# Layer 1's first two input tiles as split products in banks of their own, two buffers for turned powers, an output product that waits block by block, and a GLU tile loaded ahead of the moves

## The chip, the cores and the metric

The kernel runs on one core of one Trainium2 chip. The metric is the device time of one execution in microseconds (us); the median over several executions is what counts. A change of under 0.3% is taken here as one that a measurement of this kernel can't tell from none.

## What is computed

Two layers of a diffusion backbone over 256 latent tokens with a prefix of 256 context tokens, model width 1024, everything in f32. Cut to what matters here:

```python
for l in range(2):
    a = rmsnorm(h, norm1_g[l]) * (1 + sc1) + sh1          # context and latent tokens
    p = a @ w_in[l]                                       # columns: fourier | ssm | gate a | gate b
    y_ssm = s5_branch(p_ssm)                              # diagonal complex scan, both directions
    y_a = fourier_mix(p_fourier) @ w_four
    y_b = (y_ssm @ w_glu_a) * sigmoid(y_ssm @ w_glu_b)
    h = h + g1 * ((sigmoid(p_ga) * y_a + sigmoid(p_gb) * y_b) @ w_out)
    f = rmsnorm(h, norm2_g[l]) * (1 + sc2) + sh2
    h = h + g2 * (swiglu(f) if l == 0 else moe_top2_of_8(f))
out = rmsnorm(h, final_g)
```

In layer 1 the context tokens only feed the scan's starting state, so there the scan input is computed for all 512 tokens and everything else for the 256 latent ones.

## The kernel before, in words

Activations lie transposed: features on the partitions, 512 tokens along the row (`NT`), in eight blocks of 128 features (`KD`). Every dense product makes one block of 128 output features for all tokens in one PSUM bank, with up to eight matmuls that add up over the input blocks. Each engine has one hand-written instruction list, and semaphores join them; nothing is ordered by a scheduler. `dense(...)` and `side(...)` at the top of `program` give each product a bank and a turn, and `place`, `bank_for`, `arrived` and `taken` turn these into semaphore waits.

**Loads.** SP issues the weight tiles (2 MB each) in the order of the list `stream` into a ring of three slots. A tile may be issued once the last product that used the tile three places before it is done (`ring_load`, `last_use`). The list `moves` is `stream` with the reshaping moves that go through DRAM in between: `pack_load` (the scan input, written to `uds` by ACT in `stage_u`, read back in another layout into `pack`), `toep_load`, and `ys_move` (scan output from `stage` to `yds` and back into `pack`). SP is one queue in order: a wait of one entry holds up all that follow.

**Two kinds of product.** `product` multiplies f32 by f32; the trace shows two matmul instructions for each such matmul. `split_product`, used in layer 0's feed-forward part, takes a tile apart into a high part (ACT copies it rounded to fp32r, `weights_high`, into `FWH`) and the rest (DVE subtracts, `weights_low`, into `ringl`, which lies on the same memory as the ring slot), does the same with the activations (`aTh`, and `aTl` on the memory of `aT`), and adds three products: high by high, high by low, low by high, one matmul instruction for each. `FWH` has two buffers.

**Layer 1's head.** After layer 0's last residual, PE sums the squares (`sums`), ACT takes the root, DVE inverts, PE spreads it (`inverse_rows`); DVE scales the eight blocks (`norm`) and ACT adds the shift (`shift`). Then PE makes "u" (scan input, tile `w_in` 1, 512 columns) and "f" (Fourier input, tile `w_in` 0, 256 columns) with `product`, block after block; ACT copies each block of u out and stores it to `uds`. When all four are stored, SP issues the eight `pack` loads and then `bp` 1, the second of two tiles of turned powers. PE next makes the scan's E blocks from `pack` with `bp` 0 (blocks 0 and 1) and `bp` 1 (blocks 2 and 3), then the Fourier transforms, the gates ga and gb, the scan output Y, `ya`, `glub`, `glua` and `out`. DVE scans after the E blocks.

**Turned powers.** Layer 1's `bp` tiles are made in layer 0 among the `ya` products: DVE makes a set of powers (`in_powers`), PE transposes it (`turn`, L1595), ACT copies it from two banks into `BWs` (`turned`, L696) and stores it to `bps` (L701). There are eight sets and one `BWs`, so ACT waits before each set until the store before it has landed. ACT's next work behind the eighth set is the evacuation of layer 0's `glub` products, which alternate between two banks. `out_powers` on DVE (L1182) waits for all eight stores, since its buffer lies on the memory of `BWs`.

**Output product.** DVE mixes the two branches block by block (`mix_ready`, L1349 to L1353); PE waits for all eight mixed blocks before the first `out` matmul.

```python
                pe.wait_ge(mix_ready, 8 * l + 8)
                for h in range(2):
                    w = slot(("w_out", l, h))[:].rearrange("p (k c) -> p k c", k=KD)
```

After layer 1's `out` comes the expert part, about half of the time, which the change doesn't touch.

Of the kernel before, what the change touches and what calls it, by code (L numbers as in the profile page):

```python
# [22 lines left out]
F32 = mybir.dt.float32  # L23
# [82 lines left out]
def program(nc, a, out, bps, cks, gds, uds, yds):  # L106

    top = ExitStack()
    with top:
# [48 lines left out]
        bw_stored = sem("bw_stored")  # L158
# [15 lines left out]
        a_high = sem("a_high")  # L174
        w_high = sem("w_high")
# [47 lines left out]
        for part, size in enumerate(PARTS):  # L223
            for m in range(part * PARTS[0], part * PARTS[0] + size):
# [3 lines left out]
        dense([("ss", 1, 0), ("inv", 1, 0)] + blocks_of(1, ("u", "f", "ga", "gb", "ya", "glub", "glua", "out")) + [("ss", 1, 1), ("inv", 1, 1)],  # L228
              (0, 1, 2, 3))
# [53 lines left out]
        stream += [("toep", 1, 0), ("ck", 1, 0), ("ck", 1, 1), ("w_four", 1, 0), ("ys", 1, 0), ("ys", 1, 1)]  # L283
        stream += [("w_glu_b", 1, 0), ("w_glu_a", 1, 0), ("w_out", 1, 0), ("w_out", 1, 1)]
# [65 lines left out]
        work1.close()  # L350
        BP0 = sb(mix, "BP0", [P, 2, 4, P])
# [19 lines left out]
        prep.close()  # L371
        H = sb(mix, "H", [P, NCH + 1, 2, 32])
# [147 lines left out]
        def _(sp):  # L520
            sp.dma_start(silu_c[:], a["cT"]).then_inc(cond_in, 16)
            sp.dma_start(con[:, 0:C_FIRST], a["con"][:, 0:C_FIRST]).then_inc(con_in, 16)
            def ring_load(key):
# [12 lines left out]
                if key[0] == "bp":  # L536
                    sp.wait_ge(bw_stored, 16 * 4 * (key[2] + 1))
# [101 lines left out]
        def _(act):  # L639
# [29 lines left out]
            def masked(l, n):  # L669
# [9 lines left out]
                if l == 1 and n == 1:  # L679
                    act.wait_ge(bw_stored, 16 * ITS)  # L680
# [7 lines left out]
            def turned(l, n):  # L688

                mh, q = n // 4, n % 4  # L690
                if l == 1 and n:
                    act.wait_ge(bw_stored, 16 * n)
                for r in range(2):
                    bank, free = arrived(act, ("turn", l, n, r))
                    dst = GR[:, SLOT * mh + D * q:SLOT * mh + D * q + D] if l == 0 else BWs[:].rearrange("p g r c -> p (g r c)")
                    nc.scalar.activation(dst.rearrange("p (g r c) -> p r g c", g=4, r=2)[:, r],  # L696
                                         bank.rearrange("p (g c) -> p g c", g=4), ACT.Copy).then_inc(free, 1)
                if l == 1:
                    for r in range(2):
                        taken(act, ("turn", l, n, r))  # L700
                    act.dma_start(bps[mh][:, D * q:D * q + D], BWs[:].rearrange("p g r c -> p (g r c)"))\  # L701
                        .then_inc(bw_stored, 16)
# [54 lines left out]
            def weights_high(i):  # L757

                if i >= len(ffn_tiles):
                    return  # L760
                if i >= 2:

                    _, done, _, at, _ = place(last_use[ffn_tiles[i - 2]])
                    act.wait_ge(done, at + 1)
                n_ = stream_at[ffn_tiles[i]]
                act.wait_ge(landed[n_ % RING], 16 * (n_ // RING + 1))
                w_ = tile_src(ffn_tiles[i]).shape[-1]
# [6 lines left out]
            def shift(l, n_):  # L774

                lo = CTX if (l, n_) == (1, 1) else 0
                split = (l, n_) == (0, 1)
                for kk in range(KD):
# [5 lines left out]
                    last.then_inc(a_high if split else a_ready, 1)  # L784

            for l in range(DEPTH):
# [78 lines left out]
                if l == 0:  # L865
                    ahead = 2
                    for part, size in enumerate(PARTS):
# [14 lines left out]
                        for t in range(4):  # L882
                            weights_high(ahead)
# [93 lines left out]
        def _(dve):  # L977
# [183 lines left out]
            def out_powers(l, n):  # L1161
# [9 lines left out]
                if n == 1:  # L1171
# [3 lines left out]
                    if l == 1:  # L1175
                        dve.wait_ge(bw_stored, 16 * ITS)
# [55 lines left out]
            def norm(l, n_):  # L1232
# [13 lines left out]
                if (l, n_) == (0, 1):  # L1246

                    for kk in range(KD):
                        dve.wait_ge(a_high, kk + 1)
                        for s_ in range(2):  # L1250
                            v = slice(256 * s_, 256 * s_ + 256)
                            last = V.scalar_tensor_tensor(aTl[:, kk, v], aT[:, kk, v], modv[:, 0, 24 + kk, s_:s_ + 1],
                                                          aTh[:, kk, v].bitcast(F32), ALU.add, ALU.subtract)
                        last.then_inc(a_ready, 1)
                    weights_low(1)

            def weights_low(i):

                if i < len(ffn_tiles):
                    s_, w_ = stream_at[ffn_tiles[i]] % RING, tile_src(ffn_tiles[i]).shape[-1]  # L1260
                    dve.wait_ge(w_high, i + 1)
                    V.tensor_tensor(ringl[s_][:, 0:w_], ring[s_][:, 0:w_], FWH[i % 2][:, 0:w_].bitcast(F32),  # L1262
                                    ALU.subtract).then_inc(w_low, 1)
# [19 lines left out]
            for l in range(DEPTH):  # L1283
# [84 lines left out]
                if l == 0:  # L1368
# [4 lines left out]
                    for part, size in enumerate(PARTS):  # L1373
# [12 lines left out]
                        for m in range(8):  # L1386
                            residual(("down" + str(part), l, m), l, m, 40, 0, part == 1)
                            if m % 2:
                                weights_low(ahead)
# [166 lines left out]
        def _(pe):  # L1556
# [117 lines left out]

            for l in range(DEPTH):
# [7 lines left out]
                w = (slot(("w_in", 1, 1))[:] if l else GR[:, SLOT:2 * SLOT]).rearrange("p (k c) -> p k c", k=KD)  # L1683
                for m in range(4):
# [436 lines left out]
```

## Time and profile before

| | |
|---|---|
| Median of 3 runs | 2120.39 us (2117.6 to 2124.95) |
| The profiled execution: its own time, its span | 2125.61 us, 2123.7 us |
| Engines' busy time | PE 2046.3 us (96%), DVE 1372.9 (65%), ACT 919.8 (43%) |
| Before the experts (0 to 1118.2) | PE busy 1057.9 us |
| Experts (1118.2 to the end) | 1005.5 us, of which PE is busy 988.4 |
| Data moved | 529 MB, mean 249 GB/s |

PE is the busiest engine nearly everywhere, so the time is PE's work at the clock it is granted, and the gaps in between. A gap in a row is what stands in brackets: idle time in us before that group of instructions, and what ended it. An engine name with a q (SPq, ACTq) is its queue of DMA issues. PEclk is the granted clock as a share of the full 2.4 GHz; 0.50 is 1.2 GHz.

### The profile page before, as it was taken

What the parts mean: (1) busy time and instruction counts of PE and PEld (TensorE: products, weight loads), DVE (VectorE), ACT (ScalarE), POOL (GpSimd) and SP (SyncE); (2) the same over time, 40 slices, a digit from 0 to 9 for tenths busy, and PEclk for the clock granted to TensorE, in tenths of its full rate; (3) what the DMA queues carried; (4) which work ended last, traced back from release to release, by engine and by line L of the source; (5) the groups of instructions that cost most, each with busy time, mean ns of one, the idle gap of its engine ahead of it and who ended that gap; (6) DMA issues with size and microseconds to landing.
All of it is one profiled execution on the core that took longest, in us unless ns stands there. A gap on an engine that the chain in (4) does not pass through costs nothing.

```text
span 2123.7 us, 24374 instructions
## 1 busy us (share of the span) xinstructions
PE 2046.3 (96%) x10010; PEld 1532.1 (72%) x10010; DVE 1372.9 (65%) x1845; ACT 919.8 (43%) x839; POOL 0.2 (0%) x4
## 2 busy tenths in 40 slices
PE   5999898999999999999988999999999999999998
PEld 2446363447777777678877888888888888888886
DVE  6675635562222323336138888898988889898987
ACT  2202112121221221111116777677776776777775
POOL 0000000000000000000000000000000000000000
PEclk8999999999999999999988999999999999999999
DMA  9432784332435441368526999899998999989994
GB/s 402 84 154 100 192 244 174 125 118 84 194 139 218 159 154 67 127 189 190 187 119 239 377 352 377 333 362 375 355 374 326 375 361 365 374 325 378 353 373 181
DMA packets 83838, 529.27 MB, mean 249 GB/s; under 512 B 23056, under 2 KB 49552, under 8 KB 52752
## 3 DMA queue, kind: packets, MB, share of 16 engines
q1 hardware_dynamic: 62976, 508.65, 65.1%
q10 hardware_dynamic: 20752, 19.05, 2.6%
q8 instruction: 82, 1.34, 0.2%
q14 instruction: 28, 0.23, 0.0%
HBM read 509.39 MB, written 18.28 MB: 248 GB/s over the span
## 4 chain that ended last, share of the span: by engine, by line
PE 90%; DMA 4%; DVE 3%; ACT 1%; issue 1%; SPq 1%; DVEq 0%; ACTq 0%
PE ps L1628 21%; PE ps L1985 14%; PE ps L1970 14%; PE ps L1971 14%; PE ps L1637 6%; PE ps L1641 6%; PE ps L1644 6%; PE ps L1571 2%; DMA bps<-BWs 2%; PE ps L1792 1%; PE ps L1916 1%; DMA ring<-in_w_mod 1%; PE ps L1800 1%; PE ps L1899 1%; DVE WL L1453 1%; PE ps L1925 1%
## 5 line engine op out<-in xcount | busy, mean ns | idle before, releaser
L1453 DVE TENSOR_TENSOR WL<-mring,WH 128x2048 fp32r<-128x2048 f32 x336 | 755.1, 2287 | 105.2 <-ACT WH L903 105.0
L903 ACT ACTIVATE WH<-mring 128x2048 fp32r<-128x2048 f32 x336 | 626.1, 1913 | 139.0 <-PE ps L1985 120.7
L1970 PE MATMUL ps<-WH,XGh 128*128 128x512 f32 x896 | 355.0, 396 | 2.4 <-ACT WH L903 2.4
L1971 PE MATMUL ps<-WH,XGl 128*128 128x512 f32 x896 | 350.6, 391 | 0.0
L1628 PE MATMUL ps<-aT,ring 128*128 128x512 f32 (+1 forms) x704 | 243.5, 506 | 2.0 <-ACT aT L782 2.0
L1985 PE MATMUL ps<-WL,XGh 128*128 128x512 f32 x896 | 221.6, 389 | 0.0
L1628 PEld LDWEIGHTS ps<-aT,ring 128*128 128x128 f32 x704 | 134.9, 193 | 105.5 <-issue 95.4
L1970 PEld LDWEIGHTS ps<-WH,XGh 128*128 128x128 f32 x896 | 168.9, 188 | 36.6 <-issue 2.5
L1971 PEld LDWEIGHTS ps<-WH,XGl 128*128 128x128 f32 x896 | 169.0, 189 | 33.9
L1985 PEld LDWEIGHTS ps<-WL,XGh 128*128 128x128 f32 x896 | 168.2, 188 | 34.9
L1262 DVE TENSOR_TENSOR ringl<-ring,FWH 128x4096 fp32r<-128x4096 f32 (+2 forms) x19 | 73.4, 3863 | 182.9 <-ACT FWH L768 182.9
L768 ACT ACTIVATE FWH<-ring 128x4096 fp32r<-128x4096 f32 (+2 forms) x19 | 60.6, 3187 | 271.8 <-DMA ring<-in_ffn_gu 166.2
L1970 PE MATMUL ps<-WH,hTh 128*128 128x512 f32 x448 | 175.9, 393 | 0.0
L1971 PE MATMUL ps<-WH,hTl 128*128 128x512 f32 x448 | 174.5, 390 | 0.0
L1985 PE MATMUL ps<-WL,hTh 128*128 128x512 f32 x448 | 110.7, 389 | 0.0
L1970 PEld LDWEIGHTS ps<-WH,hTh 128*128 128x128 f32 x448 | 84.2, 188 | 17.1
L1971 PEld LDWEIGHTS ps<-WH,hTl 128*128 128x128 f32 x448 | 84.2, 188 | 17.0
L1985 PEld LDWEIGHTS ps<-WL,hTh 128*128 128x128 f32 x448 | 83.9, 188 | 17.2
L1637 PE MATMUL ps<-aTh,FWH 128*128 128x512 f32 x352 | 93.5, 405 | 2.0 <-ACT aTh L782 2.0
L1641 PE MATMUL ps<-aTl,FWH 128*128 128x512 f32 x352 | 93.0, 403 | 0.0
L1628 PE MATMUL ps<-pack,ring 128*128 128x512 f32 (+1 forms) x256 | 86.1, 496 | 6.4 <-ACT aT L755 4.7
L1644 PE MATMUL ps<-aTh,ringl 128*128 128x512 f32 x352 | 90.7, 402 | 0.0
(263 smaller groups left out, 2116.9 us busy)
## 6 DMA issues: line engine op xcount, KB each, us to landing
mring<-in_moe_gate SPq DMA_DIRECT2D x56, 2048.0 KB, 9.8
mring<-in_moe_up SPq DMA_DIRECT2D x56, 2048.0 KB, 9.6
mring<-in_moe_down SPq DMA_DIRECT2D x56, 2048.0 KB, 9.6
ring<-in_w_mod SPq DMA_DIRECT2D x23, 2048.0 KB, 8.0
ring<-in_w_in SPq DMA_DIRECT2D x11, 2048.0 KB, 11.5
ring<-in_ffn_gu SPq DMA_DIRECT2D x11, 2048.0 KB, 10.9
cks<-CW ACTq DMA_DIRECT2D x16, 512.0 KB, 3.1
ring<-cks SPq DMA_DIRECT2D x4, 2048.0 KB, 12.6
```

The costliest lines, as they stand in the source:

```text
L768: nc.scalar.activation(FWH[i % 2][:, 0:w_], ring[n_ % RING][:, 0:w_], ACT.Copy).then_inc(w_high, 1)
L903: nc.scalar.activation(WH[buf][:, o], mring[t % MRING][:, o], ACT.Copy).then_inc(high_done, 1)
L1262: V.tensor_tensor(ringl[s_][:, 0:w_], ring[s_][:, 0:w_], FWH[i % 2][:, 0:w_].bitcast(F32), ALU.subtract).then_inc(w_low, 1)
L1453: V.tensor_tensor(WL[buf][:, o], mring[t % MRING][:, o], WH[buf][:, o].bitcast(F32), ALU.subtract).then_inc(low_done, 1)
L1571: last = mm(ps[g:g + 8, 2, :], silu4[:, k, t % 4, :], wv[:, k, :], start=(t % 4 == 0 and k < 4), stop=(t % 4 == 3 and k >= 4), skip_group_ ...
L1628: last = mm(bank[:, 0:cols], w, x, start=(k == 0), stop=(k == len(pairs) - 1))
L1637: mm(bank, wh[:, k, :], xh[:, k, :], start=(k == 0), stop=False)
L1641: mm(bank, wh[:, k, :], xl[:, k, :], start=False, stop=False)
L1644: last = mm(bank, wl[:, k, :], xh[:, k, :], start=False, stop=(k == n - 1))
L1970: mm(out_, ah, WH[buf][:, o:o + 512], start=(first and q == 0), stop=False)
L1971: mm(out_, al, WH[buf][:, o:o + 512], start=False, stop=False)
L1985: last = mm(out_, ah, WL[buf][:, o:o + 512], start=False, stop=(final and q == len(pairs) - 1))
```

## The change

It has four parts.

1. **u and f of layer 1 as split products.** The two tiles join `split_tiles`: u's tile is split into high and low within the feed-forward part (index 19), f's after the shift (index 20). `shift(1, 0)` writes `aTh` and not `aT`, then copies the 256 latent columns with the shift into a new f32 buffer `aT2`, which the gates ga and gb read. DVE then writes `aTl` over `aT` (16 instructions) and splits f's tile. PE runs `split_inputs`: for u, high by high over all four banks with the input block as the outer loop, then low weights, then low activations; for f, high by high the same way, high by low, low weights last. All four banks must be free before each. The sum of squares and the inverse root of layer 1's first norm use banks 6 and 7, so that banks 0 to 3 are free for u.
2. **Two buffers for turned powers.** `BW1` beside `BWs`; each has its own store semaphore, and set n waits for the store of set n-2.
3. **Output product per mixed block.** The first `out` product of each layer waits for mixed block k before matmul k.
4. **GLU tile ahead of moves.** In layer 1 `w_glu_b` stands in front of the two `ys` moves in SP's list.

```diff
-        dense([("ss", 1, 0), ("inv", 1, 0)] + blocks_of(1, ("u", "f", "ga", "gb", "ya", "glub", "glua", "out")) + [("ss", 1, 1), ("inv", 1, 1)],
-              (0, 1, 2, 3))
+        dense([("ss", 1, 0), ("inv", 1, 0)], (6, 7))
+        dense(blocks_of(1, ("u", "f", "ga", "gb", "ya", "glub", "glua", "out")), (0, 1, 2, 3))
+        dense([("ss", 1, 1), ("inv", 1, 1)], (2, 3))
...
+        split_tiles = ffn_tiles + [("w_in", 1, 1), ("w_in", 1, 0)]
...
-        stream += [("toep", 1, 0), ("ck", 1, 0), ("ck", 1, 1), ("w_four", 1, 0), ("ys", 1, 0), ("ys", 1, 1)]
-        stream += [("w_glu_b", 1, 0), ("w_glu_a", 1, 0), ("w_out", 1, 0), ("w_out", 1, 1)]
+        stream += [("toep", 1, 0), ("ck", 1, 0), ("ck", 1, 1), ("w_four", 1, 0), ("w_glu_b", 1, 0), ("ys", 1, 0), ("ys", 1, 1)]
+        stream += [("w_glu_a", 1, 0), ("w_out", 1, 0), ("w_out", 1, 1)]
...
+                BW = (BWs, BW1)[n % 2]
-                if l == 1 and n:
-                    act.wait_ge(bw_stored, 16 * n)
+                if l == 1 and n >= 2:
+                    act.wait_ge(bw_stored[n % 2], 16 * (n // 2))
...
+                if (l, n_) == (1, 0):
+                    for kk in range(KD):
+                        nc.scalar.activation(aT2[:, kk, :], aT[:, kk, CTX:NT], ACT.Identity,
+                                             bias=modv[:, 1, kk, 1:2]).then_inc(a_copied, 1)
+                    weights_high(len(split_tiles) - 1)
...
-                if (l, n_) == (0, 1):
+                if (l, n_) in ((0, 1), (1, 0)):
                     for kk in range(KD):
-                        dve.wait_ge(a_high, kk + 1)
+                        dve.wait_ge(a_high, KD * l + kk + 1)
+                        if l:
+                            dve.wait_ge(a_copied, kk + 1)
...
+            def split_inputs():
+                for name, i in (("u", len(ffn_tiles)), ("f", len(ffn_tiles) + 1)):
+                    t0 = CTX if name == "f" else 0
+                    pe.wait_ge(w_high, i + 1)
+                    wh = FWH[i % 2][:].rearrange("p (k c) -> p k c", k=KD)
+                    wl = ringl[stream_at[split_tiles[i]] % RING][:].rearrange("p (k c) -> p k c", k=KD)
+                    banks = [bank_for(pe, (name, 1, m)) for m in range(4)]
+                    for k in range(KD):
+                        pe.wait_ge(a_high, KD + k + 1)
+                        for m in range(4):
+                            mm(banks[m][:, 0:NT - t0], wh[:, k, P * m:P * m + P], aTh[:, k, t0:NT],
+                               start=(k == 0), stop=False)
...
-                pe.wait_ge(mix_ready, 8 * l + 8)
...
                         product(("out", l, 4 * h + m),
-                                [(w[:, k, P * m:P * m + P], G[:, k, t0:NT]) for k in range(KD)], n_)
+                                [(w[:, k, P * m:P * m + P], G[:, k, t0:NT]) for k in range(KD)], n_,
+                                blocks=(mix_ready, 8 * l) if h + m == 0 else None)
```

How the instructions stand on three engines, before and now. First PE at layer 1's head; `pack,ring` 64x64 are the E blocks. Before:

```order
L1663 MATMUL ps<-rms,con 128x128 x4
L1628 MATMUL ps<-aT,ring 128x512 x32
L1628 MATMUL ps<-aT,ring 128x256 x32
L1734 MATMUL ps<-pack,ring 64x64 x128
L1628 MATMUL ps<-con,uF 128x256 x8
```

Now:

```order
L1683 MATMUL ps<-rms,con 128x128 x4
L1706 MATMUL ps<-aTh,FWH 128x512 x32
L1712 MATMUL ps<-aTh,ringl 128x512 x32
L1717 MATMUL ps<-aTl,FWH 128x512 x32
L1706 MATMUL ps<-aTh,FWH 128x256 x32
L1723 MATMUL ps<-aTl,FWH 128x256 x32
L1728 MATMUL ps<-aTh,ringl 128x256 x32
L1791 MATMUL ps<-pack,ring 64x64 x128
L1648 MATMUL ps<-con,uF 128x256 x8
```

The 32 matmuls of u and the 32 of f have become 96 each, in six groups, and the E blocks still follow f. Next ACT at the end of layer 0 and layer 1's head (FWH is a tile's high part, `stage` and `uds` are u's blocks). Before:

```order
L768 ACTIVATE FWH<-ring 128x2560 x3
L750 ACT_TABLE_LOAD
L750 ACTIVATE rms<-ps,epst 128x128
L782 ACTIVATE aT<-aT,modv 128x256 x16
L724 ACTIVATE stage<-ps 128x512
L727 DMA uds<-stage 128x512
```

Now:

```order
L778 ACTIVATE FWH<-ring 128x2560 x3
L778 ACTIVATE FWH<-ring 128x4096
L762 ACT_TABLE_LOAD
L762 ACTIVATE rms<-ps,epst 128x128
L792 ACTIVATE aTh<-aT,modv 128x256 x16
L797 ACTIVATE aT<-aT,modv 128x256 x8
L778 ACTIVATE FWH<-ring 128x4096
L736 ACTIVATE stage<-ps 128x512
L739 DMA uds<-stage 128x512
```

One tile copy stands in front of the root, eight copies and another tile copy between the shift and the first block of u. Last SP's queue in layer 1, before:

```order
L549 DMA ring<-in_w_four 128x4096
L578 DMA yds<-stage 16x16x32 x8
L581 DMA pack<-yds 128x2x256
L578 DMA yds<-stage 16x16x32 x8
L581 DMA pack<-yds 128x2x256
L549 DMA ring<-in_w_glu_b 128x4096
L549 DMA ring<-in_w_glu_a 128x4096
```

Now:

```order
L559 DMA ring<-in_w_four 128x4096
L559 DMA ring<-in_w_glu_b 128x4096
L588 DMA yds<-stage 16x16x32 x8
L591 DMA pack<-yds 128x2x256
L588 DMA yds<-stage 16x16x32 x8
L591 DMA pack<-yds 128x2x256
L559 DMA ring<-in_w_glu_a 128x4096
```

The GLU tile has moved past eighteen DMAs of the two moves.

## Rows read from the trace of the kernel before

**Rows 1.** The page's chain of work that ended last, shares by engine.
```profile
PE 90%; DMA 4%; DVE 3%; ACT 1%; issue 1%; SPq 1%; DVEq 0%; ACTq 0%
```
**Rows 2.** PE's timeline, layer 0: start, us, engine, line, instructions, [idle before <-releaser].
```profile
344.77 12.26 PE L1628 MATMUL ps<-pack,ring 128*128 128x512 f32 x24 [4.65 <-ACT aT L755]
...
371.87 27.73 PE L1628 MATMUL ps<-pack,ring 128*128 128x512 f32 x64
...
402.28 15.70 PE L1628 MATMUL ps<-G,ring 128*128 128x512 f32 x32 [1.88 <-DVE G L1353]
```
**Rows 3.** ACT's timeline, end of the turned powers.
```profile
326.45 0.33 ACTq L701 DMA_DIRECT2D bps<-BWs  x1
...
330.26 0.33 ACTq L701 DMA_DIRECT2D bps<-BWs  x1
341.30 1.09 ACT L696 ACTIVATE BWs<-ps 128x512 f32<-128x512 f32 x2 [11.12 <-DMA bps<-BWs]
```
**Rows 4.** SP's queue at that time.
```profile
329.81 0.35 SPq L549 DMA_DIRECT2D ring<-in_w_mod  x1
```
**Rows 5.** Stretches: from:to, us, busy PE, PEld, DVE, ACT, POOL (x count), PEclk, DMA share, GB/s.
```profile
344.80:348.60 3.80, 3.80 (x5) 1.60 (x6) 2.89 (x7) 0.41 (x1) 0.00 (x0) 0.55 0.01 3
...
402.30:406.30 4.00, 4.00 (x6) 1.79 (x7) 0.87 (x3) 0.00 (x0) 0.00 (x0) 0.60 0.97 412
```
**Rows 6.** DVE's timeline: a 4096-column tile's low part; layer 0's low activations.
```profile
442.52 4.42 DVE L1262 TENSOR_TENSOR ringl<-ring,FWH 128x4096 fp32r<-128x4096 f32 x1
...
473.68 6.42 DVE L1252 SCALAR_TENSOR_TENSOR aTl<-aT,modv,aTh 128x256 fp32r<-128x256 f32 x16
```
**Rows 7.** ACT's timeline: a 4096-column tile's high part; layer 1's shift.
```profile
451.60 3.62 ACT L768 ACTIVATE FWH<-ring 128x4096 fp32r<-128x4096 f32 x1 [19.14 <-DVE Gs L1200]
...
881.33 6.49 ACT L782 ACTIVATE aT<-aT,modv 128x256 f32<-128x256 f32 x16 [3.29 <-DVE aT L1241]
```
**Rows 8.** The chain in order of time: start, us, what.
```profile
499.53 1.86 PE ps L1644 x8
...
882.38 30.39 PE ps L1628 x64
913.42 2.00 DMA uds<-stage
920.33 12.90 DMA ring<-bps
...
1358.94 1.91 PE ps L1899 x16
```
**Rows 9.** PE's timeline, layer 1's head.
```profile
882.38 44.19 PE L1628 MATMUL ps<-aT,ring 128*128 128x512 f32 x128 [1.99 <-ACT aT L782]
927.11 3.95 PE L1734 MATMUL ps<-pack,ring 128*64 128x64 f32 x128 [0.55 <-DMA pack<-uds]
933.27 3.95 PE L1734 MATMUL ps<-pack,ring 128*64 128x64 f32 x128 [2.21 <-DMA ring<-bps]
```
**Rows 10.** Stretches of layer 1: its first matmuls, the wait before the second E half, Y.
```profile
882.30:887.70 5.40, 5.32 (x7) 2.25 (x8) 4.48 (x12) 5.40 (x14) 0.00 (x0) 0.50 0.00 0
...
931.10:933.20 2.10, 0.00 (x0) 0.00 (x0) 0.69 (x1) 0.00 (x0) 0.00 (x0) 1.00 1.15 484
...
1003.00:1014.00 11.00, 11.00 (x161) 10.83 (x160) 0.00 (x0) 1.77 (x3) 0.00 (x0) 1.00 0.53 192
```
**Rows 11.** PE's timeline, layer 1's GLU and output products.
```profile
1040.71 27.89 PE L1628 MATMUL ps<-pack,ring 128*128 128x256 f32 x128 [1.70 <-DMA ring<-in_w_glu_b]
1070.30 27.89 PE L1628 MATMUL ps<-G,ring 128*128 128x256 f32 x128 [1.69 <-DVE G L1353]
```
**Rows 12.** SP's queue around the ys moves of layer 1.
```profile
1014.63 4.64 SPq L578 DMA_DIRECT2D yds<-stage  x8
...
1031.99 0.38 SPq L581 DMA_DIRECT2D pack<-yds  x1
1032.42 0.47 SPq L549 DMA_DIRECT2D ring<-in_w_glu_b  x1
```

More of the change, by code:

```diff
@@ L157, in program @@
         powers_made = sem("powers_made")
-        bw_stored = sem("bw_stored")
+        bw_stored = [sem(f"bw_stored{i}") for i in range(2)]
         c_made = sem("c_made")
@@ L350, in program @@
         work1.close()
+        later = ExitStack()
+        aT2 = sb(later, "aT2", [P, KD, SEQ])
+        later.close()
         BP0 = sb(mix, "BP0", [P, 2, 4, P])
@@ L536, in ring_load @@
                 if key[0] == "bp":
-                    sp.wait_ge(bw_stored, 16 * 4 * (key[2] + 1))
+                    for b in range(2):
+                        sp.wait_ge(bw_stored[b], 16 * 2 * (key[2] + 1))
                 if key[0] == "ck":
@@ L1673, in _ @@
             inverse_rows(0, 0)
+            def split_inputs():
[10 more added lines that the diff above has]
+                               start=(k == 0), stop=False)
+                    if name == "u":
+                        pe.wait_ge(w_low, i + 1)
+                        for m in range(4):
+                            for k in range(KD):
+                                mm(banks[m][:, 0:NT - t0], wl[:, k, P * m:P * m + P], aTh[:, k, t0:NT],
+                                   start=False, stop=False)
+                        for m in range(4):
+                            for k in range(KD):
+                                pe.wait_ge(a_ready, 2 * KD + k + 1)
+                                last = mm(banks[m][:, 0:NT - t0], wh[:, k, P * m:P * m + P], aTl[:, k, t0:NT],
+                                          start=False, stop=(k == KD - 1))
+                            last.then_inc(dense_done, 1)
+                    else:
+                        for m in range(4):
+                            for k in range(KD):
+                                mm(banks[m][:, 0:NT - t0], wh[:, k, P * m:P * m + P], aTl[:, k, t0:NT],
+                                   start=False, stop=False)
+                        pe.wait_ge(w_low, i + 1)
+                        for m in range(4):
+                            for k in range(KD):
+                                last = mm(banks[m][:, 0:NT - t0], wl[:, k, P * m:P * m + P], aTh[:, k, t0:NT],
+                                          start=False, stop=(k == KD - 1))
+                            last.then_inc(dense_done, 1)
             for l in range(DEPTH):
@@ L1764, in _ @@
                             product((name, l, 4 * h + m),
[L1765 removed]
+                                    [(w[:, k, P * m:P * m + P], aT2[:, k, :] if l else aT[:, k, :]) for k in range(KD)], n_)
                             if l == 0 and h == 0:
```

59 lines of the change are left out of this document (33 added, 26 removed).

## The prediction

> **What bounds the kernel now.** I read the page first. Nine tenths of the chain that ended last are PE's [rows 1], so an edit pays if it shortens PE's work, closes a gap in it, or keeps its clock up. PE's timeline then shows the gaps that the change touches: 4.65 us before layer 0's third `glub` product and 1.88 before its `out` [rows 2]. ACT's and SP's timelines say why the first is there [rows 3, 4], and the stretches behind the gaps show what they cost besides: the granted clock is 0.55 and 0.60 there, that is, mostly 1.2 GHz [rows 5]. DVE's and ACT's rows give the price of splitting a tile and the activations [rows 6, 7]. For layer 1's head I read the chain in order of time [rows 8], PE's timeline [rows 9] and the clock [rows 10]; the last gaps are in layer 1's GLU and output products [rows 11], with SP's queue beside the first of them [rows 12]. All these gaps lie on PE, in front of work that everything later waits for, so a gap that closes comes off the end. The experts behind begin when `out` is done and keep their length.
>
> **Turned powers: 6.5 us.** The eighth store is issued at 330.26 behind SP's 2 MB load of 329.81 [rows 3, 4], and lands only for ACT's last copy at 341.30; the one before it, issued at 326.45, had landed in time for a copy at 329.1. That late landing is the whole of the gap: ACT can't evacuate `glub` before its last copy is out. With two buffers the last copy (set 8) waits for the store of set 6, issued near 322, before SP's load. ACT then copies as soon as PE has transposed (about 331.2), is done at 332.4, and the first `glub` product ends at 336.6. The 4.65 us go. The half clock behind them goes too: 24 instructions take 12.26 us where at the rate of the 64-instruction row, 27.73 / 64 each, they would take 10.40, so 1.86 [rows 2, 5]. What is late next: the last store, now issued at 332.5 behind the same load, may still land near 341. DVE's `out_powers` for set 2 waits for it and takes about 4 us, so it is ready near 346; PE needs it near 354. Covered by 8 us.
>
> **Output product per block, layer 0: 2.8 us.** PE waits 1.88 us for the eighth mixed block [rows 2]. Seven matmuls of 2 x 27.73 / 64 = 0.87 us now stand in front of the one that needs it, 6.1 us of cover for 1.88, so the gap goes whole. Its half clock costs 15.70 - 13.87 = 1.83 us [rows 2, 5]. Whether so short a gap costs clock is not certain: 2.21 us later on did not (PEclk 1.00, [rows 9, 10]), so in other executions this one may not have; I count half, 0.9.
>
> **u as a split product: 5.4 us.** Before, u is 64 instructions in 30.39 us [rows 8]; at full rate 27.73 [rows 2]; the 2.66 between are the half clock from 882.4 to 887.7 [rows 10]. Now it is 96 matmuls; eight such take 1.86 us [rows 8], so 12 x 1.86 = 22.3. The start, 882.38, doesn't move: one shifted block is enough as before. The first group asks for a new block every four matmuls, 0.93 us at full clock and 1.86 at half; ACT delivers one every 2 x 6.49 / 16 = 0.81 us [rows 7]. So PE is not starved, and pays the same 2.66. Saved: 27.7 - 22.3 = 5.4. What was added lies beside this:
> - u's tile is split during the last down products. ACT takes 3.62 us [rows 7] and DVE 4.42 [rows 6], started when block 5 ends, near 861.8: done near 870. The residual of block 6 is due at 868.7 and slips by a good 1 us; block 7's is due at 875.5 and doesn't. Nothing on the path.
> - ACT: eight copies at half of 6.49, 3.2 us, and f's tile, 3.62, after the shift at 887.8, so free near 895. u's first bank is full near 902.
> - DVE: the low activations, 6.42 us [rows 6], paced by the copies, from 888 to 895; f's low tile, 4.42, to 899. PE reads the low activations from 900 on: cover 5 us, the thinnest here. If it fails, each us late is a us lost.
>
> **f as a split product: 0 us.** The nearest row for a 256-column split matmul is the gather, 16 in 1.91 us [rows 8]: 96 x 0.119 = 11.4 us, against 13.8 before. PE has to wait about 0.7 us first, since all four banks must be free and u's last block is evacuated last. But what f saves, PE waits. The chain runs from u's last block through its store (2.00 us), eight pack issues and `bp` 1 (12.90) [rows 8], rigid behind u's end (912.8 before, 907.4 now). Before, PE waits 0.55 us for the pack and 2.21 for `bp` 1 [rows 9]. Now f ends at 907.4 + 0.7 + 11.4 = 919.5, the pack is there at 927.11 - 5.4 = 921.7 and `bp` 1 at 933.27 - 5.4 = 927.9: gaps of 2.2 and 2.2. E ends exactly 5.4 us earlier, no more. DVE's scan starts from E's end and PE's work up to Y is unchanged, so that lead stays.
>
> **GLU tile ahead of the moves: 1.7 us.** PE waits 1.70 us for the tile [rows 11], which SP issues at 1032.42, after both moves [rows 12]. Its slot is free when Y's first half is done, near 1014: it is issued there and lands long before it is used at 1039. Past it come 18 DMAs. The nearest row for small DMAs behind a 2 MB load is the eighth power store, some 11 us to landing where 2.6 is usual [rows 3], so up to 8.4 us on the first move. That moves its read-back from 1020.7 to about 1029, the second move's end from 1031.99 [rows 12] to about 1036, and the data, 3 us later, to about 1039: just when PE asks. Bounds: 1.7 gained, or nothing. I take 1.7, since the first move has 11 us between Y's halves to catch up.
> The Trainium skill ("DMA: Bandwidth & Descriptors", Issuing engines are not separate DMA queues) says that DMAs of all engines run on the same 16 DMA engines and interleave; the eighth store agrees, 11 us against 2.6. By that rule the moves give up time to the tile on whichever queue it is, and the term would be nearer its lower bound.
>
> **Output product per block, layer 1: 1.7 us.** A gap of 1.69 us [rows 11] against seven matmuls of 0.43 = 3.0 us of cover. No clock was lost there.
>
> **Sum.** 6.5 + 2.8 + 5.4 + 0 + 1.7 + 1.7 = 18.1 us. The profiled execution took 2125.6 us, so it would take 2107.5. It lies 5.2 us above the median of the runs, so part of the clock terms may be its own; against the median the forecast is 2120.4 - 18.1, **2102 us**.
>
> **Rivals.**
> 1. *The wait before E costs clock.* PE's gap before E grows from 0.55 to 2.2 us, with another of 2.2 us 4 us behind it. A gap of 1.88 cost clock in layer 0; 2.21 alone did not [rows 5, 10]. If PE falls to 1.2 GHz there, the second half of E (3.95 us) doubles and about 1.8 us are lost behind it, as after the other gaps: 5.8 us less, 2108. Chance 0.14.
> 2. *The late landings stay.* If set 6's store too came behind a load, or the moves were late by more than the tile gains, the first term or the GLU's goes: 2104 to 2109. For it: two of eight stores were late. Against: SP issues only one load between 302 and 333. Chance 0.08. Together with rival 1 it would leave about 5 us, within the 0.3% (6.4 us).
> 3. *f pays as well.* If `bp` 1 lands sooner, since the loads around it lie otherwise, up to 2.4 us more: 2100. Chance 0.08.
> 4. *Switching banks keeps the clock down.* The new products change bank with every matmul in their first groups. Were PE at 1.2 GHz all through u and f, u would take 44.6 us (+14.2) and f 22.8, so that f, not `bp` 1, sets E: u's end 927.0, f's at 950.5, E's, 7.9 us at least, at 958.4 against 937.2. That is 21.2 us lost against 12.7 gained elsewhere: 2129, slower. It decides from 12.7 us lost on. Against it: Y changes between two banks with every matmul, and its clock is 1.00 over 11 us [rows 10]. Chance 0.03.
> The Trainium skill ("TensorE: Matmul & The Clock Gate", A second HAM failure mode: psum-queue depth-cycling) describes a kernel in which cycling through banks made PE idle briefly and its clock swing. That speaks against this change; Y's row doesn't bear it out.
>
> **How the numbers follow.** Forecast 0.67, rivals 0.14, 0.08, 0.08, 0.03. The range runs from 2096 (18.1 and f's 2.4, the other half of the `out` term, 0.9, and 2.66 of clock at u's start, should it be granted there) to 2110 (18.1 less 5.8, 1.7 and a little). Faster by over 0.3%: 0.94; rivals 1 and 2 together give 0.03 within it; slower 0.03.
>
> **What would show it.** Right: no gap before `glub`'s third product and none before either `out`; PEclk 1.00 behind them; u in some 25 us from the same start; the gaps before both halves of E near 2.2 us and E ending 5.4 us earlier relative to the root; no gap before layer 1's `glub`. Wrong: PEclk 0.50 beyond the first 6 us of u, PE waiting for `aTl` or for a residual before the sums, ACT still waiting for `bps` at the last set, or PE waiting for `pack<-yds`.

## The result, and the profile after

| | before | changed |
|---|---|---|
| Median | 2120.39 us (2116.09 to 2125.82, 5 runs) | 2104.91 us (2100.72 to 2107.68, 5 runs) |
| Profiled execution, span | 2125.61 us, 2123.7 us | 2107.13 us, 2105.3 us |
| Ratio | | 0.9918, 95% interval 0.9900 to 0.9936 |

The change makes the kernel 0.8% faster. The forecast was 2102 us, with a range from 2096 to 2110.

PE's timeline of the changed kernel, layer 0 (columns as in [rows 2]):

```profile
334.75 17.43 PE L1648 MATMUL ps<-pack,ring 128*128 128x512 f32 x40
...
394.59 0.95 PE L1604 MATMUL ps<-con,mrow 128*128 128x8 f32 x8
395.40 13.98 PE L1648 MATMUL ps<-G,ring 128*128 128x512 f32 x32
```

The five `glub` products that were 16 and 24 instructions with 4.65 us between [rows 2] are now one run of 40, and `out` follows the eight small matmuls without a gap, at full rate: 13.98 us for the 32 instructions that took 15.70. ACT no longer waits for a store behind the fourth set. Its timeline at the last one:

```profile
332.64 1.09 ACT L708 ACTIVATE BW<-ps 128x512 f32<-128x512 f32 x2 [3.80 <-PE ps L1615]
```

Layer 1 on PE, from the spread root to the output product:

```profile
874.00 10.11 PE L1706 MATMUL ps<-aTh,FWH 128*128 128x512 f32 x32 [2.00 <-ACT aTh L792]
883.95 7.49 PE L1712 MATMUL ps<-aTh,ringl 128*128 128x512 f32 x32
891.27 7.63 PE L1717 MATMUL ps<-aTl,FWH 128*128 128x512 f32 x32
899.78 4.07 PE L1706 MATMUL ps<-aTh,FWH 128*128 128x256 f32 x32 [0.89 <-ACT stage L736]
903.69 3.81 PE L1723 MATMUL ps<-aTl,FWH 128*128 128x256 f32 x32
907.34 3.79 PE L1728 MATMUL ps<-aTh,ringl 128*128 128x256 f32 x32
913.13 7.89 PE L1791 MATMUL ps<-pack,ring 128*64 128x64 f32 x209 [2.00 <-DMA pack<-uds]
921.62 1.61 PE L1791 MATMUL ps<-pack,ring 128*64 128x64 f32 x47 [0.61 <-issue]
923.16 3.72 PE L1648 MATMUL ps<-con,uF 128*128 128x256 f32 x16
...
1024.84 27.79 PE L1648 MATMUL ps<-pack,ring 128*128 128x256 f32 x128
1052.47 27.79 PE L1648 MATMUL ps<-G,ring 128*128 128x256 f32 x128
```

u takes 24.9 us instead of 30.4 [rows 8]. f is done 12.2 us after u, 1.6 sooner than before, and PE then stands 2.00 us for the pack. Both gaps of [rows 11] are gone.

The same stretches of PE's work in the two profiles, each from one group's start to the next one's:

| stretch | before | changed | difference | forecast |
|---|---|---|---|---|
| start to `ya` of layer 0 | 292.5 | 294.3 | +1.8 | 0 |
| `ya` to the sums before the feed-forward part | 169.7 | 159.3 | -10.4 | -9.3 |
| feed-forward part, to the sums of layer 1 | 413.2 | 413.4 | +0.2 | 0 |
| u's start to the end of E | 54.8 | 49.2 | -5.6 | -5.4 |
| E's end to Y | 65.8 | 65.8 | 0 | 0 |
| Y to `glub` | 37.8 | 35.9 | -1.9 | -1.7 |
| `glub` to `out` | 29.6 | 27.6 | -2.0 | -1.7 |
| `out`'s end to the gather | 21.5 | 19.5 | -2.0 | 0 |
| experts | 1004.0 | 1005.6 | +1.6 | 0 |

The parts that the change touches gave 19.9 us, and the parts that it doesn't touch took 1.4 us more. These scatter: over the twelve profiles of this document the first row goes from 289.3 to 294.3 us and the one that ends at the gather from 19.5 to 21.6, and before the gather the clock came back some us later or earlier (mean PEclk 0.61 before, 0.69 after). So one profile's total is good to a few us only. Most other stretches repeat to some tenths, but not the one from u's start to the end of E. With the same instructions in it, it took 49.2 us here and 49.7, 50.7, 50.5, 48.7 and 49.5 in five later profiles, 49.7 in the mean. The 5.6 us of the table are one draw between 4.0 and 6.1.

### The profile page after: what moved, and what is told of

Same layout as the page of the kernel before. It is cut to its first block, busy times and chain, and to the rows that moved or that the text cites. A ratio compares the mean times of both kernels' runs of the same rounds, so it can differ in the third digit from the quotient of the medians.

```text
span 2105.3 us, 24542 instructions
## 1 busy us (share of the span) xinstructions
PE 2036.1 (97%) x10074; PEld 1538.5 (73%) x10074; DVE 1388.0 (66%) x1863; ACT 930.3 (44%) x849; POOL 0.2 (0%) x4
## 3 DMA queue, kind: packets, MB, share of 16 engines
q1 hardware_dynamic: 62976, 508.65, 65.8%
## 4 chain that ended last, share of the span: by engine, by line
PE 92%; DVE 4%; DMA 2%; ACT 1%; issue 1%; SPq 0%; DVEq 0%; ACTq 0%
PE ps L1648 20%; PE ps L2044 14%; PE ps L2029 14%; PE ps L2030 14%; PE ps L1657 6%; PE ps L1661 6%; PE ps L1664 6%; PE ps L1591 2%; PE ps L1851 1%; PE ps L1975 1%; DMA ring<-in_w_mod 1%; PE ps L1791 1%; PE ps L1859 1%; PE ps L1958 1%; DVE WL L1473 1%; PE ps L1615 1%
## 5 line engine op out<-in xcount | busy, mean ns | idle before, releaser
L1281 DVE TENSOR_TENSOR ringl<-ring,FWH 128x4096 fp32r<-128x4096 f32 (+2 forms) x21 | 82.2, 3917 | 185.9 <-ACT FWH L778 185.9
L1648 PE MATMUL ps<-aT,ring 128*128 128x512 f32 (+1 forms) x576 | 200.1, 507 | 0.0
L2029 PEld LDWEIGHTS ps<-WH,XGh 128*128 128x128 f32 x896 | 169.3, 189 | 36.7 <-issue 2.5
L778 ACT ACTIVATE FWH<-ring 128x4096 fp32r<-128x4096 f32 (+2 forms) x21 | 67.9, 3232 | 283.4 <-DMA ring<-in_ffn_gu 166.2
L1648 PEld LDWEIGHTS ps<-aT,ring 128*128 128x128 f32 x576 | 110.0, 193 | 85.4 <-issue 78.7
L1657 PEld LDWEIGHTS ps<-aTh,FWH 128*128 128x128 f32 x352 | 66.8, 192 | 26.8 <-issue 9.0
## 6 DMA issues: line engine op xcount, KB each, us to landing
ring<-cks SPq DMA_DIRECT2D x4, 2048.0 KB, 12.2
```

Of the source, the lines that this page charges most:

```text
L778: nc.scalar.activation(FWH[i % 2][:, 0:w_], ring[n_ % RING][:, 0:w_], ACT.Copy).then_inc(w_high, 1)
L1648: last = mm(bank[:, 0:cols], w, x, start=(k == 0), stop=(k == len(pairs) - 1))
L1657: mm(bank, wh[:, k, :], xh[:, k, :], start=(k == 0), stop=False)
L2029: mm(out_, ah, WH[buf][:, o:o + 512], start=(first and q == 0), stop=False)
```

## The experiments

All are the changed kernel with one edit, if nothing else is said, and each was timed in five rounds beside the kernel before. The changed kernel's 2104.91 us come from another job than theirs, and the kernel before itself had medians from 2120.39 to 2124.59 us in the four jobs. So each difference from the changed kernel is given twice, between the medians and between the ratios to the kernel before. Both are good to a few us only; the stretch in the profile decides what a part is worth.

**One buffer for the turned powers.**

```diff
-                BW = (BWs, BW1)[n % 2]
-                if l == 1 and n >= 2:
-                    act.wait_ge(bw_stored[n % 2], 16 * (n // 2))
+                BW = BWs
+                if l == 1 and n:
+                    act.wait_ge(bw_stored[(n - 1) % 2], 16 * ((n + 1) // 2))
```

> The changed kernel with one buffer for the turned powers again (each copy waits for the store before it). Theory: the wait of ACT for the late eighth store comes back, PE stands some 4.5 us before layer 0's third glub product and then runs at 1.2 GHz for 3 to 4 us, so the kernel is 6 to 6.5 us slower than the changed one (2104.9 us), near 2111. Rival: the late store would have been covered by what the other parts moved, and nothing comes back: near 2105.

Measured: 2110.64 us, 0.9936 (0.9911 to 0.9962), 5.7 us above the changed kernel, 3.8 by the ratios. PE's and ACT's timelines of this kernel:

```profile
346.08 13.44 PE L1648 MATMUL ps<-pack,ring 128*128 128x512 f32 x24 [5.54 <-ACT aT L767]
```
```profile
331.32 0.33 ACTq L713 DMA_DIRECT2D bps<-BWs  x1
342.60 1.08 ACT L708 ACTIVATE BWs<-ps 128x512 f32<-128x512 f32 x2 [11.37 <-DMA bps<-BWs]
```

The store issued at 331.32 holds the last copy until 342.60, PE stands 5.54 us, and the 24 instructions behind take 13.44 us where 10.40 is full rate. In this profile that is 8.6 us, in the one of before 6.5: the size moves with where the load falls. The cause is as forecast.

**All blocks before the output product.**

```diff
+                pe.wait_ge(mix_ready, 8 * l + 8)
                 for h in range(2):
...
-                                blocks=(mix_ready, 8 * l) if h + m == 0 else None)
```

> The changed kernel with both layers' output products waiting for all eight mixed blocks again. Theory: PE stands 1.9 us in layer 0 and 1.7 us in layer 1; with the half clock that followed the first gap in the kernel before (1.8 us) that is 3.6 to 5.5 us, so 2108.5 to 2110.4. The profile tells whether the clock falls again behind a gap as short as 1.9 us: the theory of the prediction holds that it does in some executions only. Rival: the clock falls always, and the difference is 5.4 us.

Measured: 2109.1 us, 0.9933 (0.9915 to 0.9950), 4.2 us above the changed kernel, 3.2 by the ratios. Its PE timeline in layer 0 and layer 1, and the clock behind the first gap (columns as in [rows 5]):

```profile
393.18 15.59 PE L1648 MATMUL ps<-G,ring 128*128 128x512 f32 x32 [1.88 <-DVE G L1372]
...
1054.75 27.89 PE L1648 MATMUL ps<-G,ring 128*128 128x256 f32 x128 [1.70 <-DVE G L1372]
```
```profile
393.00:397.00 4.00, 3.82 (x5) 1.70 (x6) 1.07 (x4) 0.00 (x0) 0.00 (x0) 0.57 0.96 408
```

Both gaps return at the length they had, and the clock falls behind the first as it did before (0.57, and 0.60 in [rows 5]) and not behind the second. In both profiles that have this gap it cost clock: 1.88 + 1.61 + 1.70 = 5.2 us in all.

**u and f as plain products.** This is the kernel before with the other three parts, so the diff of the change without its first part.

> The kernel before with three of the four parts (two buffers, product per block, GLU tile ahead), so u and f of layer 1 are plain f32 products. Theory: against the changed kernel it lacks the 5.4 us of u and nothing for f, so E ends 54.8 us after u's start and not 49.2, and the time is near 2110.3. Rival: f's saving counts as well and the difference is 7.8 us, near 2112.7. Second rival: the split costs something elsewhere (DVE, ACT, the last residuals) and the difference is under 3 us.

Measured: 2110.73 us, 0.9939 (0.9921 to 0.9956), 5.8 us above the changed kernel, 4.5 by the ratios. PE's timeline:

```profile
871.05 44.17 PE L1635 MATMUL ps<-aT,ring 128*128 128x512 f32 x128 [2.00 <-ACT aT L788]
915.72 3.95 PE L1741 MATMUL ps<-pack,ring 128*64 128x64 f32 x128 [0.50 <-DMA pack<-uds]
...
925.82 3.72 PE L1635 MATMUL ps<-con,uF 128*128 128x256 f32 x16
```

From u's start to E's end it takes 54.8 us, the changed kernel 49.2 in its first profile and 49.7 in the mean of six. That is all that part 1 gives, 5.1 us in the mean; the first rival, 7.8 us, is out. The second is out too: the feed-forward part takes 413.3 us here and 413.4 in the changed kernel, so splitting u's tile cost nothing there. That the gain is u's and not f's is shown next.

**f as a plain product.** u stays split; f reads the f32 copy `aT2` and the unsplit tile, and the tile's high and low parts are left out.

```diff
-                    weights_high(len(split_tiles) - 1)
...
-                    weights_low(len(split_tiles) - 1 if l else 1)
+                    if l == 0:
+                        weights_low(1)
...
-                for name, i in (("u", len(ffn_tiles)), ("f", len(ffn_tiles) + 1)):
+                for name, i in (("u", len(ffn_tiles)),):
...
+                        product(("f", 1, m), [(wf[:, k, P * m:P * m + P], aT2[:, k, :]) for k in range(KD)], n_)
```

> The changed kernel with f as a plain f32 product from the latent copy of the activations and the unsplit tile; u stays split. Theory: f ends about 13.9 us after u and meets the pack, which comes 14.3 us after it: a gap of 0.4 us, so PE's clock stays at 2.4 GHz through E, where in the changed kernel a gap of 2.0 us put it at 1.2 GHz for 3.8 us. E's second half then waits for bp 1, 18.9 us after u's end or a little later. E's end relative to u's end moves by -1.5 to 0 us, and the kernel is as fast as the changed one or up to 1.5 us faster: 2103.4 to 2105. Rival: splitting f pays on its own, and this kernel is 2.4 us slower, near 2107.3.

Measured: 2103.99 us, 0.9907 (0.9887 to 0.9926), 0.9 us below the changed kernel, 2.3 by the ratios, within the scatter. PE's timeline, and the clock over E's first half:

```profile
869.17 9.89 PE L1706 MATMUL ps<-aTh,FWH 128*128 128x512 f32 x32 [2.00 <-ACT aTh L792]
...
893.69 13.98 PE L1648 MATMUL ps<-aT,ring 128*128 128x256 f32 x64
908.60 3.95 PE L1795 MATMUL ps<-pack,ring 128*64 128x64 f32 x128 [0.92 <-DMA pack<-uds]
913.23 3.60 PE L1795 MATMUL ps<-pack,ring 128*64 128x64 f32 x114 [0.68 <-DMA ring<-bps]
917.18 0.68 PE L1795 MATMUL ps<-pack,ring 128*64 128x64 f32 x14 [0.36 <-issue]
917.79 3.72 PE L1648 MATMUL ps<-con,uF 128*128 128x256 f32 x16
```
```profile
908.00:913.00 5.00, 3.95 (x128) 3.81 (x128) 2.48 (x4) 0.09 (x1) 0.00 (x0) 1.00 1.03 439
```

E ends 48.6 us after u's start, 0.5 sooner than in the changed kernel's first profile and 1.1 sooner than in the mean of its six. The same stretch there reads

```profile
913.00:915.00 2.00, 1.87 (x42) 1.88 (x44) 0.26 (x1) 0.00 (x0) 0.00 (x0) 0.67 1.01 434
915.00:917.00 2.00, 2.00 (x44) 2.00 (x42) 0.98 (x2) 0.00 (x0) 0.00 (x0) 0.50 1.00 426
```

so its gap of 2.00 us put PE at 1.2 GHz over E's first half. The wait for `bp` 1 was small by then. The tile landed 10.1 us after its issue and not 12.9 as before, at 917.7; by my estimate the first half would have ended at 913.13 + 3.95 = 917.1 at full clock, and the second half would have waited 0.6 us. It started at 918.5, so the slow clock cost some 0.7 us. Splitting f pays nothing: what it saves turns into a wait for the pack, a slower clock and a stop inside E (last section).

**The GLU tile behind the moves.**

```diff
-        stream += [..., ("w_four", 1, 0), ("w_glu_b", 1, 0), ("ys", 1, 0), ("ys", 1, 1)]
-        stream += [("w_glu_a", 1, 0), ("w_out", 1, 0), ("w_out", 1, 1)]
+        stream += [..., ("w_four", 1, 0), ("ys", 1, 0), ("ys", 1, 1)]
+        stream += [("w_glu_b", 1, 0), ("w_glu_a", 1, 0), ("w_out", 1, 0), ("w_out", 1, 1)]
```

> The changed kernel with layer 1's first GLU tile behind the two moves in SP's queue again. Theory: PE stands 1.7 us before layer 1's first glub product, nothing else changes, near 2106.7. The profile shows besides what the moves gain when no tile is ahead of them: in the changed kernel the first move's read-back was issued 9.7 us after its first store, in the kernel before 6.1. Rival: the moves were held up by the tile and PE's gain is less than 1 us.

Measured: 2108.13 us, 0.9936 (0.9912 to 0.9960). The timing is 3.2 us above the changed kernel, 3.8 by the ratios, more than this part can give: PE's gap is 0.66 us, and 1.3 us more lie between u's start and E's end, where the edit changes nothing. SP's queue around the moves, first this kernel, then the changed one:

```profile
999.43 3.80 SPq L588 DMA_DIRECT2D yds<-stage  x8
1004.68 0.38 SPq L591 DMA_DIRECT2D pack<-yds  x1
1010.49 3.77 SPq L588 DMA_DIRECT2D yds<-stage  x8
1015.67 0.38 SPq L591 DMA_DIRECT2D pack<-yds  x1
1016.10 0.47 SPq L559 DMA_DIRECT2D ring<-in_w_glu_b  x1
```
```profile
1000.12 0.33 SPq L559 DMA_DIRECT2D ring<-in_w_glu_b  x1
1000.63 6.08 SPq L588 DMA_DIRECT2D yds<-stage  x8
1010.36 0.38 SPq L591 DMA_DIRECT2D pack<-yds  x1
...
1016.89 0.38 SPq L591 DMA_DIRECT2D pack<-yds  x1
```

The first read-back follows the first store by 5.3 us here and by 9.7 with the tile in front: the tile costs the first move 4.5 us, of the 8.4 that were the bound. The second move absorbs it. Counted from Y's start, its read-back is issued 27.9 us later in both kernels, and `glub` starts after 36.7 and 35.9 us. Part 4 is worth 0.8 us by this pair and 1.9 by before and after. The 1.1 us between them are not the tile's. In the kernel before, the stores of the second move took longer to issue:

```profile
1025.69 4.87 SPq L578 DMA_DIRECT2D yds<-stage  x8
```

One of the eight took 1.54 us where the others take at most 0.46, and the read-back was issued 29.0 us after Y's start. With plain u and f it was 1.45 us for one store and 28.9; in all ten profiles with a split u, 27.9 or 28.0. So part 1 had already taken 1.1 us of this gap away; why those stores are quicker with it stays open.

The Trainium skill ("DMA: Bandwidth & Descriptors", Issuing engines are not separate DMA queues) has the DMAs of all engines run on the same 16 DMA engines and interleave; the 4.5 us agree, and the move had the slack for it.

**u block by block.** The bank is the outer loop now and the input block the inner one, and the three groups of a bank follow one another.

```diff
-                    for k in range(KD):
-                        pe.wait_ge(a_high, KD + k + 1)
-                        for m in range(4):
+                        for m in range(4):
+                            for k in range(KD):
+                                pe.wait_ge(a_high, KD + k + 1)
```

> The changed kernel with u's split product written block after block (eight matmuls in a row for one bank) instead of the input block outside and the bank inside. Theory: PE's first eight matmuls are then paced by ACT's shift (0.81 us each and not 0.23), so the first group takes 6.3 us instead of 1.9 to 3.7 and the clock stays at 1.2 GHz far longer, as at the start of layer 0's feed-forward part (469 to 484 us in the kernel before). u takes 30 to 33 us instead of 24.9 and the kernel is 5 to 8 us slower, 2110 to 2113. Rival (the rule on cycling through banks): bank after bank costs clock, so this order is as fast or faster.

Measured: 2107.95 us, 0.9948 (0.9928 to 0.9967), 3.0 us above the changed kernel, 6.4 by the ratios. PE's timeline:

```profile
868.64 6.28 PE L1707 MATMUL ps<-aTh,FWH 128*128 128x512 f32 x8 [2.00 <-ACT aTh L792]
...
879.48 0.50 PE L1715 MATMUL ps<-aTl,FWH 128*128 128x512 f32 x1 [0.29 <-DVE aTl L1271]
...
923.02 3.72 PE L1648 MATMUL ps<-con,uF 128*128 128x256 f32 x16
```

The first eight matmuls take 6.28 us, paced by ACT, the last of the third group wait for DVE, and E ends 54.4 us after u's start. That is 5.2 us more than in the changed kernel's first profile, 3.6 to 5.7 more over its six, and 0.4 less than with plain products. The order is what makes the split pay: the split in this order gives nearly nothing.

The Trainium skill ("TensorE: Matmul & The Clock Gate", A second HAM failure mode: psum-queue depth-cycling) describes a kernel that cycles through PSUM banks and whose clock swings, since PE idles briefly between its groups. The changed kernel changes bank with every matmul of u's first group and doesn't idle there: once the clock is back the matmuls start every 0.227 us at a granted clock of 1.00. So the change of bank by itself cost no clock here, and the version that stays in one bank is the slower one.

**Fourier transforms before E.** The list of side products and PE's code have the first transforms ahead of the pack's wait.

```diff
+        side([("dft1", 1, m, t) for m in range(4) for t in range(2, 4)])
         side([("E", 1, m, d) for m in range(4) for d in range(2)])
-        side([("dft1", 1, m, t) for m in range(4) for t in range(2, 4)]
-             + [("dft2", 1, m, 1) for m in range(4)])
+        side([("dft2", 1, m, 1) for m in range(4)])
```

> The changed kernel with the first Fourier transforms of layer 1 (eight products of one f32 matmul, 3.5 us) moved ahead of the E blocks, into the wait for the pack. Theory: the gap of 2.0 us before E is filled and PE's clock does not fall in E; E ends about where it did or 1 us later, and the 3.5 us are gone from behind it. DVE's scan has 4.3 us of slack before Y and loses the 3.5 us: it may just become the bound. Gain 2 to 3.5 us against the changed kernel: 2101.4 to 2103. Rival: the scan or bp 1 becomes the bound and nothing is gained.

Measured: 2104.44 us, 0.9915 (0.9890 to 0.9940), 0.5 us below the changed kernel, 0.6 by the ratios: no gain. PE's timeline:

```profile
906.90 3.61 PE L1648 MATMUL ps<-con,uF 128*128 128x256 f32 x16
910.45 5.81 PE L1800 MATMUL ps<-pack,ring 128*64 128x64 f32 x191
918.35 2.96 PE L1800 MATMUL ps<-pack,ring 128*64 128x64 f32 x65 [2.09 <-issue]
921.24 8.00 PE L1648 MATMUL ps<-con,GR 128*128 128x256 f32 x32
```

The gap before E is filled, and neither the scan nor `bp` 1 took its place. A stop of 2.09 us inside E did, and the clock fell behind it: 8.00 us for 32 instructions that take 7.07. From u's end to the gates it is 34.3 us against 34.7. A miss, and of a kind that I had not thought of (last section).

**The first feed-forward tile in u's order.** `split_product` for its four products gives way to the order of `split_inputs`, and the sums and root before it go to banks 6 and 7.

```diff
+            def first_tile(wh, wl):
+                parts = [(bank_for(pe, (name, 0, m)), u, m) for m in range(2) for u, name in enumerate(("gate", "up"))]
+                for k in range(KD):
+                    pe.wait_ge(a_high, k + 1)
+                    for bank, u, m in parts:
+                        mm(bank, wh[:, u, k, P * m:P * m + P], aTh[:, k, :], start=(k == 0), stop=False)
...
+        dense([("ss", 0, 1), ("inv", 0, 1)], (6, 7))
```

> The changed kernel with the first tile of layer 0's feed-forward part (gate and up of blocks 0 and 1) made in the order that the change uses for u: input block outside, four banks inside, low weights second and low activations last; the sum of squares and the inverse root before it go to banks 6 and 7. Theory: these four products take 31.7 us in the kernel before, since ACT's shift and DVE's low part pace the first one and the clock stays at 1.2 GHz for 15 us; in the order of u they take 24.9 as u does in the changed kernel. Gain 6.8 us: near 2098. Rival: the work behind them (ACT's evacuation, DVE's low tile) is late then and takes half of it back: near 2101.5.

Measured: 2098.67 us, 0.9893 (0.9870 to 0.9916), 6.2 us below the changed kernel, 5.3 by the ratios. PE's timeline of the changed kernel, then of this one:

```profile
460.55 6.29 PE L1657 MATMUL ps<-aTh,FWH 128*128 128x512 f32 x8 [2.00 <-ACT aTh L792]
466.63 5.72 PE L1661 MATMUL ps<-aTl,FWH 128*128 128x512 f32 x8
472.15 3.62 PE L1664 MATMUL ps<-aTh,ringl 128*128 128x512 f32 x8
...
492.83 2.00 PE L1657 MATMUL ps<-aTh,FWH 128*128 128x512 f32 x8
```
```profile
458.22 9.02 PE L1701 MATMUL ps<-aTh,FWH 128*128 128x512 f32 x32 [1.99 <-ACT aTh L793]
...
481.87 2.00 PE L1658 MATMUL ps<-aTh,FWH 128*128 128x512 f32 x8
```

The four products take 23.7 us instead of 32.3, and nothing is given back: up to layer 1's sums it is 397.7 us against 406.5.

**Both together, and the changed kernel beside it.** The edits of the last one and of f as a plain product, and in the same job the changed kernel once more, unaltered.

> The changed kernel with both edits that gained or cost nothing: the first feed-forward tile in the order of u, and f as a plain f32 product. Theory: the first gives 8.6 us, as its four products took 23.7 us in its own run against 32.3 in the changed kernel; the second gives 0 to 1 us, since E ends 48.6 us after u's start and not 49.2. Together near 2096 to 2098, 7 to 9 us below the changed kernel in the same job. Rival: the runs of other jobs were lucky ones and the difference is under 5 us.

> The changed kernel once more, unaltered, on the chip and in the rounds of the version above, so that the two can be compared without the kernel before between them. Theory: 2102 to 2107, and 0.990 to 0.994 of the kernel before. Its profile shows which of the short losses are there in every execution: the clock at 1.2 GHz in E's first half behind a gap of 2 us, and the stop at E's 209th matmul instruction, which stood in all five profiles with a split f.

Measured in the same job: 2098.25 us, 0.9892 (0.9871 to 0.9913), and for the changed kernel 2105.9 us, 0.9930 (0.9908 to 0.9952). The combined version is 7.7 us faster than the changed kernel and 22.2 faster than the one before. Its stretch up to layer 1's sums is 399.1 us against 406.4, a gain of 7.3; its first tile had the clock back 5.8 us after its start, the version above after 3.2. Against the version with the new tile order alone it gains nothing that can be told, so f's split can go for simplicity and not for time. The changed kernel's second profile has both short losses again, the slow clock over E's first half (7.88 us for the 209 instructions) and the stop behind it:

```profile
912.58 7.88 PE L1791 MATMUL ps<-pack,ring 128*64 128x64 f32 x209 [2.15 <-DMA pack<-uds]
921.25 1.62 PE L1791 MATMUL ps<-pack,ring 128*64 128x64 f32 x47 [0.79 <-issue]
```

## Why the prediction was right, step by step

- **Turned powers, 6.5 us forecast.** Together with layer 0's output product the stretch gave 10.4 us. Undoing it gave 5.7 us in the timing, 3.8 by the ratios, and 8.6 in the profile. Mechanism right: the store of set 6 was in time, and the last store, again behind the load, hurt nobody.
- **Output product, 2.8 and 1.7 us.** The gaps went whole. The step "I count half, 0.9" was too small: the clock fell behind the 1.88 us gap in both profiles that have one, so the term is 3.5 us. The length of a gap doesn't tell what it costs. The gaps before E's first half, 1.88 to 3.10 us in the seven profiles with f split and in front of E, all cost clock too; 1.69 and 1.70 before `glub` and `out` and 2.21 and 2.26 before E's second half did not. The first gap stands behind 0.95 us of eight small matmuls; whether that is the reason was not tried.
- **u, 5.4 us.** u itself went from 30.4 to 24.9 us, 5.5. Over the stretch it is 5.6 in the first profile, and 4.0 to 6.1 over six, so that this figure came so near is partly luck. The start, the first 6 us at 1.2 GHz and the covers held: the first three groups followed one another without a wait, the residual slipped (861.5 instead of 860.2) and the sums didn't.
- **f, 0 us.** Right in value, and the gap before the pack came as worked out (2.00 us for 2.2); the rest is partly luck. The step that failed is "gaps of 2.2 and 2.2": there is no second gap. The forecast had `bp` 1 land 12.90 us after its issue, as before; it landed after 10.1, so at full clock 0.6 us of that wait would have been left. That is rival 3's condition, and still nothing more was gained. Rival 1's first half happened, the clock fell to 0.50 over E's first half, and cost some 0.7 us, since the clock was back for the second half. Then came a stop of 0.61 us inside E that no term and no rival had. These losses used up what the early tile gave.
- **GLU tile, 1.7 us.** 1.9 by before and after, 0.8 by undoing it; the other 1.1 came with part 1. The bound of 8.4 us for the first move was twice what it cost, 4.5.
- **The sum.** 18.1 us forecast; 19.9 in the touched stretches of the profiles, 15.5 between the medians, 17.4 by the ratio (13.6 to 21.2 by its interval). The rest is scatter of this kernel. Rival 4 (the change of bank with every matmul keeps the clock down) is out: the clock came back 5.5 us after u's start, as it did before (5.4), in the middle of the group that changes banks. PEclk is 0.50 up to 879 us, and then (columns as in [rows 5])

```profile
880.00:881.00 1.00, 1.00 (x7) 0.80 (x5) 1.00 (x3) 1.00 (x4) 0.00 (x0) 1.00 0.00 0
```

## What to carry to other kernels

A product whose inputs are still being made should run its input blocks in the outer loop and as many banks as are free in the inner one: each new block then feeds four matmuls, the pace of its maker is covered, and the clock comes back early. It gave 7.3 and 8.8 us on the first feed-forward tile and 3.6 to 5.7 on u. Before an instruction group is made faster, follow what stands behind its end; where a chain of transfers hangs on the group before it, as the pack does on u, the time saved only becomes a wait. And price a gap with the clock behind it, but only where the slower work is itself on the path.

## What the runs showed that I had not expected

PE stops inside E at a fixed place of its instruction list, waiting for no semaphore that the profile shows ("issue"). With f split it is behind E's 208th or 209th matmul instruction in seven profiles (0.61, 0.79, 0.17, 0.88, 1.92, 1.09 and 0.66 us). With the 16 instructions of the transforms moved in front it is behind the 191st (2.09 us), and with a plain f, 64 instructions and not 96, behind the 242nd and 241st (0.36 and 0.42 us). So the place moves with the number of instructions before it, and the length varies from execution to execution.

The profile shows more than that. Its table of DMA queues has a queue q8 of kind "instruction", 81 packets of 16 KB in the changed kernel, about one for every 250 of PE's matmuls and weight loads. The table for the window from 919.30 to 919.36 us of the changed kernel, 1.7 us before the stop, reads (packets, MB, share of the 16 engines)

```profile
q8 instruction: 1, 0.02, 112.0%
```

In all ten profiles with a stop the latest such packet starts 0.35 to 2.2 us before it, and PE goes on 2.3 to 2.5 us after the packet's start, whether the stop is 0.17 or 2.09 us long. That fits PE waiting for its own instructions. It also shows where the gain of the moved transforms went: PE goes on 48.2 us after u's start with them in front, and 47.1 to 49.2 in the six profiles without them. What sets the packet's own time is open, and no run was made to move it. The DMA engines are fully busy there with bulk loads (share 0.89 to 1.09 over stretches of 2 us); no run changed the loads. In the kernel before, and with plain u and f, such a packet starts 2.6 us before E's second half, within the wait for `bp` 1, so no stop is seen. And the slow store of the second `ys` move in these same two kernels runs while a q8 packet does (from 1026.03 and 1015.75 us).

The other surprise is how long the kernel before stays slow at the first feed-forward tile. With matmuls paced by ACT at 0.8 us each and then by DVE at 0.7, PE has 1.2 GHz for some 16 us, where back-to-back work from the same start had the clock back after 3.2 and 5.8.
